# Swapping rotated channels on VectorE's lanes instead of on TensorE, with retention's tables, the routing's splits and the release of expert weights moved

## What is computed

```python
def apply_rotary(t, cos, sin):
    t1, t2 = jnp.split(t.astype(jnp.float32), 2, axis=-1)
    return jnp.concatenate([t1 * c - t2 * s, t1 * s + t2 * c], axis=-1)

# attention: 24 heads of 64 for q and for k, rotated; retention: 8 heads of 64, rotated
q_a = apply_rotary(q_a.reshape(B, S, n_a, HEAD_DIM), cos, sin)
k_a = apply_rotary(k_a.reshape(B, S, n_a, HEAD_DIM), cos, sin)
q_r = apply_rotary(q_r.reshape(B, S, RET_HEADS, RET_QK_DIM), cos, sin)
k_r = apply_rotary(k_r.reshape(B, S, RET_HEADS, RET_QK_DIM), cos, sin) * RET_QK_DIM ** -0.5
# retention: scores times exp(distance * log_g), forwards and backwards
...
hn = rms_norm_2(h, norm_moe_w)              # router logits = hn @ w_group, hn @ w_expert
# best of 8 groups, best 2 of its 8 experts; for each expert:
hid = jax.nn.silu(xb @ w1[e]) * (xb @ w3[e])
return hid @ w2[e]
```

## Time and profile before

| | us |
|---|---|
| median of 3 runs | 3439.86 |
| lowest, highest | 3435.97, 3440.55 |
| the profiled execution, its own time | 3437.58 |
| its span in the trace | 3435.7 |
| TensorE busy | 3219.6 (94%) |
| VectorE busy | 1311.5 (38%) |
| ACT busy | 886.7 (26%) |
| POOL busy | 130.6 (4%) |

### The profile page before, as it was taken

One profiled execution on the slowest core, in us unless ns is written; L12 is line 12 of the kernel. 1 busy time (PEld: TensorE's weight loads), 2 busy tenths in 40 slices (PEclk: granted clock), 3 DMA queues, 4 the chain that ended last, 5 costly groups with the idle time before them and its releaser, 6 DMA issues.

```text
span 3435.7 us, 35738 instructions
## 1 busy us (share of the span) xinstructions
PE 3219.6 (94%) x15116; PEld 2219.2 (65%) x15116; DVE 1311.5 (38%) x2183; ACT 886.7 (26%) x1420; POOL 130.6 (4%) x122
## 2 busy tenths in 40 slices
PE   9999999999999999998999989998989999999895
PEld 7678688887678688886888867777434334334332
DVE  5775633335675543334343344534311111111112
ACT  3452232222352332222333432322111111111111
POOL 0000000001000000001101000001000000000001
PEclk9999999999999999999999999999999999999997
DMA  4122122333122123332211321125799999999996
GB/s 171 51 93 90 62 86 92 98 106 110 62 74 99 51 98 97 103 112 68 68 56 58 98 74 56 56 98 207 293 426 425 426 426 426 426 425 426 426 426 263
DMA packets 229541, 627.62 MB, mean 183 GB/s; under 512 B 14784, under 2 KB 136512, under 8 KB 179968
## 3 DMA queue, kind: packets, MB, share of 16 engines
q1 hardware_dynamic: 207888, 581.47, 43.8%
q10 hardware_dynamic: 19296, 35.68, 2.9%
q0 software_dynamic: 2192, 8.13, 0.8%
HBM read 600.32 MB, written 22.81 MB: 181 GB/s over the span
## 4 chain that ended last, share of the span: by engine, by line
PE 68%; DMA 17%; DVE 10%; ACT 2%; POOL 2%; issue 1%; ACTq 0%; SPq 0%; DVEq 0%; POOLq 0%
PE bank L121 66%; DMA piece_high<-in_moe_w 4%; DMA piece<-in_moe_w 3%; DMA mT_slot<-in_moe_w 3%; DMA xT<-in_moe_w 3%; DVE gate_acc L139 2%; PE bank L124 2%; DVE x_tok L139 2%; POOL root L136 1%; DMA y_att_slot<-in_moe_w 1%; DMA memT<-in_moe_w 1%; DMA norm_room<-in_moe_w 1%; DVE stat L154 1%; DVE piece_rounded L136 1%; ACT piece_high_rounded L127 1%
## 5 line engine op out<-in xcount | busy, mean ns | idle before, releaser
L121 PE MATMUL bank<-xT_rounded,piece_high_rounded 128*128 128x512 f32 (+1 forms) x1408 | 549.8, 390 | 6.2 <-DVE xT_low_rounded L136 6.2
L136 DVE TENSOR_TENSOR piece_rounded<-piece,piece_high_rounded 128x2048 fp32r<-128x2048 f32 (+1 forms) x156 | 342.5, 2199 | 555.2 <-ACT piece_high_rounded L127 555.1
L121 PE MATMUL bank<-xT_rounded,piece_rounded 128*128 128x512 f32 (+1 forms) x1408 | 538.0, 382 | 0.0
L121 PE MATMUL bank<-xT_low_rounded,piece_high_rounded 128*128 128x512 f32 (+1 forms) x1408 | 534.1, 379 | 0.0
L136 DVE TENSOR_TENSOR gate_and_hidden<-gate_and_hidden,bank 64x512 f32<-64x512 f32 x64 | 69.2, 1081 | 821.9 <-ACT gate_and_hidden L127 821.9
L127 ACT ACTIVATE piece_high_rounded<-piece 128x2048 fp32r<-128x2048 f32 (+1 forms) x156 | 283.4, 1820 | 260.2 <-DMA piece<-in_ffn_w_down 102.7
L121 PEld LDWEIGHTS bank<-xT_rounded,piece_high_rounded 128*128 128x128 f32 x1408 | 265.8, 189 | 61.7 <-DVE xT_low_rounded L136 7.4
L121 PEld LDWEIGHTS bank<-xT_low_rounded,piece_high_rounded 128*128 128x128 f32 x1408 | 265.5, 189 | 55.5 <-issue 4.1
L121 PEld LDWEIGHTS bank<-xT_rounded,piece_rounded 128*128 128x128 f32 x1408 | 264.3, 188 | 56.4
L121 PE MATMUL bank<-piece,xeT 128*64 128x512 f32 x488 | 236.0, 637 | 17.0 <-DMA xT<-in_moe_w 6.6
L121 PE MATMUL bank<-piece_high,xeT 128*64 128x512 f32 x464 | 186.5, 639 | 14.6 <-DMA piece<-in_moe_w 8.9
(11 more groups left out here) (336 smaller groups left out, 5010.9 us busy)
## 6 DMA issues: line engine op xcount, KB each, us to landing
piece<-in_moe_w SPq DMA_DIRECT2D x90, 1024.0 KB, 16.7
piece_high<-in_moe_w SPq DMA_DIRECT2D x88, 1024.0 KB, 16.5
xT<-in_moe_w SPq DMA_DIRECT2D x59, 1024.0 KB, 17.2
mT_slot<-in_moe_w SPq DMA_DIRECT2D x58, 1024.0 KB, 16.9
piece<-in_ffn_w_in SPq DMA_DIRECT2D x40, 1024.0 KB, 5.0
memT<-in_moe_w SPq DMA_DIRECT2D x30, 1024.0 KB, 16.1
y_att_slot<-in_moe_w SPq DMA_DIRECT2D x30, 1024.0 KB, 16.1
norm_room<-in_moe_w SPq DMA_DIRECT2D x29, 1024.0 KB, 16.9
```

What stands on the lines that cost most here:

```text
L121: return self.engine.matmul(*a, **k) if self.engine is not None else Nothing()
L136: return self.engine.tensor_tensor(*a, **k) if self.engine is not None else Nothing()
```

## The change

- The swap products and the matrix `swap_a` with its load are gone, in attention (24) and in retention (8). VectorE multiplies straight out of the product's bank, in four parts of 32 lanes, each reading the other half's lanes and writing its own; the sign now lies in the table of sines. In retention the part is a `scalar_tensor_tensor` with the scale of k. The bank is given back by the last part, and no more by ACT's copy. The first part waits for that copy, as POOL's multiply with cos does.
- Retention's tables 2 and 3 get their diagonal, and table 4 is made, after the first half of v in the order of VectorE and ACT.
- Routing: ACT makes `hn_high` of a tile between its evictions; the subtraction is VectorE's, tile 0 within the merge's output, tiles 1 to 3 ahead of the logits.
- Experts: after channel block 3 TensorE ticks and releases the first halves of w1 and w3; the second halves as before.

```diff
-    def rotate_pe(self, e, pair, n):
-        bank = self.banks.take(e, "a_swap", pair, n)
-        e.wait_ge(*self.at("a_raw", pair, n))
-        e.matmul(bank[:, :], self.swap_a[:, :], self.raws[(pair * 2 * NG + n) % 2], start=True, stop=True).then_inc(
-            *e.tick("pe", "a_swap", pair, n))
-        self.banks.give(("a_swap", pair, n), "a_sin", pair, n)
+    def swapped(self, b):
+        other = b + 1 - b % 2 * 2
+        return slice(b * 32, (b + 1) * 32), slice(other * 32, (other + 1) * 32)
...
     def rotate_dve(self, e, pair, n):
-        e.wait_ge(*self.at("pe", "a_swap", pair, n))
+        bank = self.bank("a_qk", pair, n)
+        e.wait_ge(*self.at("pe", "a_qk", pair, n))
         e.wait_ge(*self.at("a_tables", "sin"))
-        e.tensor_tensor(buf, self.bank("a_swap", pair, n)[:, :], self.sin_a, ALU.mult).then_inc(*e.tick("a_sin", pair, n))
+        e.wait_ge(*self.at("a_raw", pair, n))
+        for b in range(4):
+            to, other = self.swapped(b)
+            e.tensor_tensor(buf[to, :], bank[other, :], self.sin_a[other, :], ALU.mult).then_inc(
+                *(e.tick("a_sin", pair, n) if b == 3 else e.tick()))
...
     def rotate_pool(self, e, pair, n):
-        e.wait_ge(*self.at("pe", "a_swap", pair, n))
+        e.wait_ge(*self.at("a_raw", pair, n))
...
     def item_pe(self, e, pair, item):
-            self.banks.give(("a_qk", pair, n), "a_raw", pair, n)
+            self.banks.give(("a_qk", pair, n), "a_sin", pair, n)
-            if n:
-                self.rotate_pe(e, pair, n - 1)
...
     def retention_pe(self, e):
-                banks.give((label, c4), "r_raw", label, c4)
-                bank = banks.take(e, "r_swap", label, c4)
-                e.wait_ge(*at("r_raw", label, c4))
-                e.matmul(bank[:, :], self.swap_a[:, :], self.raw_r[c4 % 2], start=True, stop=True).then_inc(
-                    *e.tick("pe", "r_swap", label, c4))
-                banks.give(("r_swap", label, c4), "r_sin", label, c4)
+                banks.give((label, c4), "r_sin", label, c4)
...
     def retention_act(self, e):
-            if label == "retention q":
-                self.decay_exp_act(e, 4)
...
+            if half == 0:
+                self.decay_exp_act(e, 4)
...
     def router_act(self, e):
             if i:
                 self.hn_turned_act(e, i - 1)
+                self.hn_high_act(e, i - 1)
         self.hn_turned_act(e, NT - 1)
-        for i in range(NT):
-            self.high_of(e, self.hn_high[:, i, :], self.hn_low[:, i, :]).then_inc(*e.tick("hn_high", i))
+        self.hn_high_act(e, NT - 1)
+
+    def hn_split_dve(self, e, i):
+        e.wait_ge(*self.at("pe", "hnT", i, 4))
+        e.wait_ge(*self.at("hn_high", i))
+        self.low_of(e, self.hn_low[:, i, :], self.hn_low[:, i, :], self.hn_high[:, i, :]).then_inc(*e.tick("hn_split", i))
...
     def hidden_pe(self, e, n, wg, wu, first=()):
+            if k == KD // 2 - 1 and first:
+                ins.then_inc(*e.tick())
+                for piece in first:
+                    self.release(e, piece)
```

More of the change, by code:

```diff
@@ L271, in memory @@
         self.ident = self.sb("ident", [P, P])
-        self.swap_a = self.sb("swap_a", [P, P])
         self.swap_q = self.sb("swap_q", [P, P])
@@ L828, in setup_act @@
                                ("freq", self.freq, a["c_freq"]), ("cols", self.cols[:, :], a["cols"]),
-                               ("swap_q", self.swap_q[:, :], a["c_swap_q"]), ("mask_q", self.mask_q, a["c_mask_q"]),
-                               ("swap_a", self.swap_a[:, :], a["c_swap_a"])):
+                               ("swap_q", self.swap_q[:, :], a["c_swap_q"]), ("mask_q", self.mask_q, a["c_mask_q"])):
             e.dma_start(dst, src).then_inc(*e.lands("setup_loads", "setup_landed", name))
@@ L858, in angles_dve @@
         angle, turns = self.angle, self.turns
-        e.wait_ge(*self.at("setup_landed", "swap_a"))
+        e.wait_ge(*self.at("setup_landed", "mask_q"))
         e.tensor_copy(angle, self.pos_i).then_inc(*e.tick())
@@ L1799, in item_pe @@
             self.release(e, self.held)
-        if n == 0:
-            self.rotate_pe(e, pair, 2 * NG - 1)
     def item_act(self, e, pair, item):
@@ L2168, in retention_dve @@
                     self.dve_piece(e, label)
-                e.wait_ge(*at("pe", "r_swap", label, c4))
-                e.tensor_tensor(buf[c4], self.bank("r_swap", label, c4)[:, :], self.sin_r, ALU.mult).then_inc(
-                    *e.tick("r_sin", label, c4))
+                e.wait_ge(*at("pe", label, c4))
+                e.wait_ge(*at("r_raw", label, c4))
+                for b in range(4):
+                    to, other = self.swapped(b)
+                    e.scalar_tensor_tensor(out=buf[c4][to, :], in0=self.bank(label, c4)[other, :],
+                                           scalar=RQK ** -0.5 if label == "retention k" else 1.0,
+                                           in1=self.sin_r[other, :], op0=ALU.mult, op1=ALU.mult).then_inc(
+                        *(e.tick("r_sin", label, c4) if b == 3 else e.tick()))
                 e.wait_ge(*at("r_cos", label, c4))
@@ L2175, in retention_dve @@
                     *e.tick("r_rotated", label, c4))
-            if label == "retention q":
+        for half in range(2):
+            self.dve_piece(e, "retention v")
+            self.dve_piece(e, "retention v")
+            if half == 0:
                 self.decay_twice_dve(e, 2)
@@ L2180, in retention_dve @@
         self.decay_twice_dve(e, 4)
-        for half in range(2):
-            self.dve_piece(e, "retention v")
-            self.dve_piece(e, "retention v")
         for j in range(NT):
@@ L2332, in merge_dve, with normed @@
                     self.low_of(e, low, low, self.mT[:, c, :]).then_inc(*e.tick("m_split", c))
-        self.project_out_dve(e, "merge_out", "mixer out", KD, 1.0, False, lambda i: ("ffn1b", "normed", i),
-                             lambda i: self.rms_dve(e, i, self.hn_low[:, i, :], self.gain[:, :], "moe_norm", ("moe_norm", "gain"), KD))
+        def normed(i):
+            self.rms_dve(e, i, self.hn_low[:, i, :], self.gain[:, :], "moe_norm", ("moe_norm", "gain"), KD)
+            if i == 2:
+                self.hn_split_dve(e, 0)
+        self.project_out_dve(e, "merge_out", "mixer out", KD, 1.0, False, lambda i: ("ffn1b", "normed", i), normed)
     def router_pe(self, e):
@@ L2394, in router_act, with hn_high_act @@
                 self.hn_turned_act(e, i - 1)
+                self.hn_high_act(e, i - 1)
         self.hn_turned_act(e, NT - 1)
-        for i in range(NT):
-            self.high_of(e, self.hn_high[:, i, :], self.hn_low[:, i, :]).then_inc(*e.tick("hn_high", i))
+        self.hn_high_act(e, NT - 1)
+    def hn_high_act(self, e, i):
+        self.high_of(e, self.hn_high[:, i, :], self.hn_low[:, i, :]).then_inc(*e.tick("hn_high", i))
+    def hn_split_dve(self, e, i):
+        e.wait_ge(*self.at("pe", "hnT", i, 4))
+        e.wait_ge(*self.at("hn_high", i))
+        self.low_of(e, self.hn_low[:, i, :], self.hn_low[:, i, :], self.hn_high[:, i, :]).then_inc(*e.tick("hn_split", i))
     def hn_turned_act(self, e, i):
@@ L2412, in router_pool @@
             self.root_pool(e, i, 1, "moe_norm", i)
-        for i in range(NT):
-            e.wait_ge(*self.at("hn_high", i))
-            e.wait_ge(*self.at("pe", "hnT", i, 4))
-            self.low_of(e, self.hn_low[:, i, :], self.hn_low[:, i, :], self.hn_high[:, i, :]).then_inc(*e.tick("hn_split", i))
     def first_best(self, e, out, scores, best):
@@ L2444, in router_dve @@
         e.tensor_scalar(self.from_far, self.iota64, -1.0, FAR, ALU.mult, ALU.add).then_inc(*e.tick())
+        for i in range(1, NT):
+            self.hn_split_dve(e, i)
         e.wait_ge(*at("pe", "router"))
@@ L2575, in rows_T_pe, with hidden_pe @@
             self.banks.give(("xeT", q, half), "xeT", q, half)
-    def hidden_pe(self, e, n, wg, wu):
+    def hidden_pe(self, e, n, wg, wu, first=()):
         bank, x = self.banks.take(e, "hidden", n), self.xeT[n // 2 % 2]
@@ L2619, in experts_pe @@
                     e.wait_ge(*self.at("landed", piece))
-                self.hidden_pe(e, n - 1, [self.expert_piece(p) for p in gu[:2]], [self.expert_piece(p) for p in gu[2:]])
-                for piece in gu:
+                self.hidden_pe(e, n - 1, [self.expert_piece(p) for p in gu[:2]], [self.expert_piece(p) for p in gu[2:]],
+                               gu[0::2])
+                for piece in gu[1::2]:
                     self.release(e, piece)
@@ L2970, in constants @@
     c = {"c_ident": np.eye(P, dtype=f),
-         "c_swap_a": swap([(0, 32), (64, 32)], P),
          "c_swap_q": swap([(lo, ROPE // 2) for lo in range(0, P, ROPE)], P)}
```

3 lines of the change are left out of this document (2 added, 1 removed).

## The result

| | before | after |
|---|---|---|
| median, us | 3438.79 | 3404.85 |
| lowest, highest | 3435.97, 3440.55 | 3400.84, 3405.79 |
| span of the profiled execution | 3435.7 | 3404.0 |
| VectorE busy | 1311.5 | 1377.9 |

The ratio is 0.990, with a 95% interval of 0.9883 to 0.9917: the change gained 34 us. I had said 51 (3386, range 3379 to 3398), so the direction was right and the time lies outside the range. The sections of the two traces show where the 17 us are. Each landmark is one row of TensorE (SP's for the last); the span, from 3435.7 to 3404.0, is 31.7 us shorter, and the four sections hold 32.2.

The account below looks back on a forecast made before the run. TensorE was taken to bound the kernel up to the routing, the weight loads in the experts stage. Terms 20.4 + 21.3 + 5.9 + 3.5 = 51.1 us off 3437.6 gave 3386 us, range 3379 to 3398.

Parts of the forecast that it names:

- What bounds the kernel: Whole kernel: TensorE sets the end up to the routing; in the experts stage the weight loads do, at 426 GB/s.
- Attention, 24 swaps of 0.85: Attention: each swap product holds TensorE for 0.85 us, so removing 24 takes 20.4 us off the path.
- The price of a part: VectorE's rotation: each of four 32x512 multiplies takes 0.74 us, with 1.08 kept for the range.
- the bank that now waits for the rotation (a_sin in place of a_raw) is asked for again only some seven banks later, over 13 us: Attention: a reason given why TensorE would not feel VectorE's longer rotation.
- So VectorE lags by a few us there and regains it among v's tiles: Attention's densest place: six rotations (21.9 us) and three splits of 2.29 us stand against six products (33.1 us) plus scores.
- Cost on the path: nothing, while the lag stays under about 6 us: Attention: VectorE's longer rotations cost TensorE nothing; a step leaves about 6 us for lag.
- The prediction's own sign: Attention: the forecast is wrong if TensorE's idle rows there name a split or a bank.
- rival A: Attention and retention: VectorE's lag reaches TensorE, splits late some 4 us for each of three pairs; 3401 us, chance 0.13.
- Retention 21.3: Retention's q and k: swaps, their waits, half-clock matmuls and table 4's exponential go, saving 21.3 us.
- Routing 5.9: Routing: hn_low's split leaves POOL, so three VectorE operations before `both` run uncontended, saving 5.9 us.
- Early release 3.5: Experts: first halves of w1 and w3 given back earlier, so DMA saturation comes 3.5 us sooner.
- B to D: Only small terms fail, 3389 to 3392 (0.17); change misses the end, 3437 (0.02); VectorE bounds attention, 3445 (0.02).

Follow-up runs that it names:

- the rotation first: The changed kernel, with VectorE rotating the sixth q/k tile before making the low part of v's second piece; 3388.7 us, ratio 0.9852.

## Why the prediction was wrong, point by point

- **What bounds the kernel**: right. From the release in expert 1 to the end it takes 995.6 us before, 996.4 changed and 996.8 with the rotation first, so what is gained ahead of saturation comes out at the end, to about 1 us.
- **Attention, 24 swaps of 0.85**: right, 20.6 us, but only in the kernel with the rotation first.
- **The price of a part**: 0.74 said, 0.71 measured; VectorE busy 139 us said, 139.6 with the rotation first.
- **"the bank that now waits for the rotation (a_sin in place of a_raw) is asked for again only some seven banks later, over 13 us"**: this step failed. Seven takes it is. But the 13 us fit no step: one with two q/k products lasts 14.8 us in the changed kernel (scores at 1763.31, the next at 1778.12) and one with two v tiles 9.1 (1812.85 to 1821.97). Among v's items, and with `ay` taking one more, seven takes go by in 9.2 us (1776.7 to 1785.9).
- **"So VectorE lags by a few us there and regains it among v's tiles"** and **"Cost on the path: nothing, while the lag stays under about 6 us"**: I counted VectorE's work, and it has time enough. I didn't ask in what order it does it. The rotation stood behind the next scores' reductions and a split that waits for ACT, and VectorE sat idle 1.75 us ahead of that split with the tile lying ready. The prediction's own sign came true: TensorE's idle rows in the attention name a bank.
- **The price of a wait**: I had costed none there, and rival A's 4 us a pair were late splits. The waits are 2.0 to 2.4 us, 6.9 in all; the half clock behind them, 11.7 us in all, which neither the forecast nor A had, is the larger part. Of this part the size is no fixed price: the same three waits cost 5.1 in another execution.
- **Retention 21.3**: right (21.4). The swaps and their waits go together (19.9 with the tables in their new place), and the tables' place was needed too (3.4 in the trace, 5.5 by the medians).
- **Routing 5.9**: right to the tenth; the splits at 1.22 us, the logits not delayed. The 2.15 us of `hn_low`'s rows, which the prediction kept as another pace for the splits, belong to a call that reads its inputs eight elements apart (`KD` as its last argument); the splits read in order.
- **Early release 3.5**: right on the kernel before and with the rotation first (35.4 us from `both` to the release), but in part by luck: in the changed kernel 2.4 came, and most traces are like it. There the granted clock from expert 0's first product to the release in expert 1 is 0.79 (24.33 us), with the rotation first 0.85 (22.94 us) for the same 70 matmuls: how long half clock lasts behind the routing isn't the same from trace to trace, which the prediction had as 2 us either way.
- **Sum**: 51.1 was said. With the failed step mended by one exchanged line it is 3440.0 - 3388.7 = 51.3, and in the traces 20.6 + 27.3 + 3.5 = 51.4 from the attention's first product to the release (the spans differ by 48.7, the rest lying ahead of that product and behind the release). That the two agree to 0.3 us is closer than the runs can tell, whose spread is 6 us and more.
- **Rivals**: A's time (3401) is nearest, with 0.13, but not by its mechanism: no split came late, and VectorE was not short of time. B to D fell. The range was too narrow because it bounded the cost of a part and not that of the order.

## What to carry over

When a buffer's release moves from one operation to another, follow the new one through its engine's program: write down for each release how many takes later the buffer is wanted, in the fastest stretch and not in the usual one, and what stands ahead of the releasing operation, waits included. On a TensorE that had not waited, a new wait of 2.0 to 4.0 us cost its length and 1.7 to 5.1 us of half clock besides in these traces, once nothing (the 3.18 us in retention); one of 1.1 to 1.8 us cost its length alone. Put the larger sum into the range. And if an engine has idle time in front of the operation that others wait for, exchange two lines before taking work away.

## What the hardware did that I had not expected

- Behind each of ten waits of 2.0 to 4.0 us in the attention TensorE was granted half its clock for a time, which cost 1.7 us five times, 3.4 once and 5.1 four times. It didn't follow the wait: 2.44 us was followed by 5.1 in one trace and by 1.7, twice, in another, and the longest, 3.96, by 1.7. Behind 1.1 to 1.8 us the clock stayed, and behind 3.18 us in retention, in the middle of products of 128x512, it did too. What sets the difference is open.
- A VectorE operation that starts 0.07 us behind a subtraction on POOL took 4.13 us instead of 2.09. The 2.04 more are about one of POOL's subtractions, as if it were held for one of them and then ran at its pace; a row doesn't show which.
- Moving 32 lanes to their neighbours on VectorE's way out of PSUM cost nothing: 2.84 us for four parts with and without it.
